# Second block of a two-block kernel: latent projections, rotations and gate tiles stand beside the attention steps, and masked key chunks are left out

## What is computed

```python
h = rmsnorm(x, pre_norm_mix)
g_a, g_b, qa, ka, va, cq, ckv, kr = split(h @ w_in)        # 1024,1024,512,128,128,256,128,32
out_a = attention_a(qa, ka, va, positions, sinks)          # 8 heads of 64, 2 key heads, window 128, ALiBi, sinks
qb  = rmsnorm(cq,  q_a_norm)  @ w_q_b                      # 8 heads of 64 + 32 (rotated)
kvb = rmsnorm(ckv, kv_a_norm) @ w_kv_b                     # 8 heads of 64 keys + 64 values
out_b = causal_attention(qb, kvb, rope(kr))                # 8 heads
merged = sigmoid(g_a) * (out_a @ w_o_a) + sigmoid(g_b) * (out_b @ w_o_b)
x = x + rmsnorm(merged @ w_out, post_norm_mix)
x = x + rmsnorm(relu(rmsnorm(x, pre_norm_mlp) @ w_up)**2 @ w_down, post_norm_mlp)
```

## Time and profile before

| what | value |
|---|---|
| median of 3 runs | 1555.5 us (1555.41 to 1556.49) |
| the profiled execution | 1553.86 us, of it the span 1552.1 us |
| TensorE matmul busy | 1351.1 us (87%) |
| VectorE busy | 998.1 us (64%) |
| ScalarE busy | 546.2 us (35%) |
| GpSimd busy | 628.8 us (41%) |
| mean granted TensorE clock | 0.946 of full speed |

### The profile page before, as it was taken

The page is one execution under the profiler, slowest core; times in us unless marked ns, Lnnn a source line. Parts: engine busy times, 40 slices in busy tenths (PEclk is TensorE's granted clock), DMA queues, the critical chain, the costliest instruction groups (busy, mean ns, idle before and its releaser), DMA issues. The chain is left out here.

```text
span 1552.1 us, 26715 instructions
## 1 busy us (share of the span) xinstructions
PE 1351.1 (87%) x10416; PEld 1296.6 (84%) x10416; DVE 998.1 (64%) x2056; ACT 546.2 (35%) x984; POOL 628.8 (41%) x361
## 2 busy tenths in 40 slices
PE   7989998899898878696888787888898898799996
PEld 6989998898897878696878787888886678689996
DVE  4698946755478585858585859555647565584563
ACT  6444454444432121211112121211564464344341
POOL 1387742221365545454545454542147312122220
PEclk9999999899999989898989898999999999899998
DMA  7445452442359999999999999999342224145450
GB/s 289 148 163 189 172 200 95 163 163 102 114 232 420 422 421 422 422 422 421 422 421 421 420 421 422 422 421 421 139 138 82 82 104 141 50 156 202 164 190 27
DMA packets 58073, 397.56 MB, mean 256 GB/s; under 512 B 6272, under 2 KB 9856, under 8 KB 10368
## 3 DMA queue, kind: packets, MB, share of 16 engines
q0 software_dynamic: 36864, 268.45, 41.6%
q1 hardware_dynamic: 21120, 127.89, 23.2%
HBM read 395.27 MB, written 1.05 MB: 255 GB/s over the span
## 5 line engine op out<-in xcount | busy, mean ns | idle before, releaser
L449 POOL TENSOR_TENSOR w_lo<-raw,w_hi 128x2048 fp32r<-128x2048 f32 x62 | 287.2, 4634 | 570.8 <-ACT w_hi L903 524.2
L761 PE MATMUL bank<-h_norm,rows_late 128*128 128x128 f32 x2816 | 332.8, 281 | 27.1 <-ACT h_norm L1052 27.1
L761 PEld LDWEIGHTS bank<-h_norm,rows_late 128*128 128x128 f32 x2816 | 328.6, 198 | 30.5 <-ACT h_norm L1052 30.5
L1591 DVE SCALAR_TENSOR_TENSOR rows_late<-rows_late,squares 128x1024 f32<-128x1024 f32 x176 | 212.8, 1223 | 131.0 <-DMA rows_late<-peer_uv_dram,stage 129.3
L588 PE MATMUL bank<-x_hi_a,w_hi 128*128 128x256 f32 (+1 forms) x904 | 266.5, 295 | 20.0 <-DVE x_lo_a L1214 11.0
L589 PE MATMUL bank<-x_lo_a,w_hi 128*128 128x256 f32 (+1 forms) x904 | 258.9, 286 | 0.0
L590 PE MATMUL bank<-x_hi_a,w_lo 128*128 128x256 f32 (+1 forms) x904 | 258.9, 286 | 0.0
L761 PE MATMUL bank<-h_norm,rows_early 128*128 128x128 f32 x1280 | 179.5, 309 | 91.0 <-ACT h_norm L1052 90.9
L761 PEld LDWEIGHTS bank<-h_norm,rows_early 128*128 128x128 f32 x1280 | 173.2, 222 | 97.6 <-ACT h_norm L1052 97.6
L530 POOL DMA_INDIRECT rows_late<-peer_uv_dram,stage x165 | 195.1, 1183 | 132.7 <-PE bank L761 95.1
L903 ACT ACTIVATE w_hi<-raw 128x2048 fp32r<-128x2048 f32 (+1 forms) x119 | 224.3, 1887 | 52.7 <-PE bank L590 45.7
...
## 6 DMA issues: line engine op xcount, KB each, us to landing
...
```

The lines of the kernel that those rows point to most:

```text
L449: api.tensor_tensor(ring(w_lo, i), ring(raw, i), ring(w_hi, i).bitcast(F32), ALU.subtract).then_inc(w_lo_ready[LO_BY[i][0]], 1)
L761: mm = nc.tensor.matmul(ct(Y_ACC[c][t // 4], t % 4, P), expert_rows(k)[:, D + t * P:D + (t + 1) * P], ct(diag, k % DIAGS, P), start=False, ...
L1591: w_.scalar_tensor_tensor(out=row, in0=row, scalar=1.0, in1=h_tok[:, c * D:(c + 1) * D], op0=ALU.mult, op1=ALU.mult, accum_out=pre[:, side ...
```

## The change

1. **Masked keys.** Scores, bias, exponentials and probabilities cover 384 columns instead of 512: 128 keys for the first token chunk, 256 for the second (`SEEN`, `SEEN_BY`). Three transposes instead of four; the second value matmul has 128 columns instead of 256.
2. **Order.** The attention loop starts after the first two `qa` tiles. Beside it stand, by step: 0 `ckv`, `kr`; 1 the other two `qa`; 2 the mean square of the key latent and `cq`; 3 `kn`, `vb`; 4 the mean square of the query latent, the rotation of `kr` and two gate tiles; 5 `qb`; 6 to 9 two query rotations each; 6 to 15 one gate tile each; 16 to 18 the last four gate tiles. The two mean squares are output tiles now, and their roots (`root_of_lora`) stand among the exponentials.
3. **Normalising.** ScalarE multiplies the probabilities by the inverse sums (`normalise`) instead of VectorE (L1459).
4. **Low parts.** VectorE makes the low parts of all weight blocks from `ka` up to the last gate block; 9 of them were GpSimd's. GpSimd keeps the ALiBi bias.
5. **Residual.** Scaling the second token chunk's residual (L1681, L1637) moves from the start of the block to step 15.

```diff
+SEEN = 3 * P
...
+ROTATED = {6: 0, 7: 2, 8: 4, 9: 6}
+GATE_TILES = {4: (0, 1), 16: (12, 13), 17: (14,), 18: (15,), **{i: (i - 4,) for i in range(6, 16)}}
...
-    p.append(("w_in_2_tail", 0, [("ckv", 0), ("kr", 0)], "act"))
-    add("w_in_2", [11], "cq", 2, "act")
-    add("w_in_2", [8, 9], "qa", 2, "act")
-    p.append(("w_kv_b_2", 0, [("kn", i) for i in range(HB)] + [("vb", i) for i in range(4)], "act"))
-    other("krot", 1, "dve")
-    p.append(("w_q_b_2", 0, [("qb", i) for i in range(HB)], "act"))
+    add("w_in_2", [8], "qa", 2, "act")
     for i in range(HA + HB + 3):
         if i >= 3:
             other(("apv", "bpv")[(i - 3) // HA], 1, "dve", (i - 3) % HA)
-        if i < HB:
-            other("qrot", 1, "dve", i)
-        if i % 2 == 0 and i < 16:
-            add("w_in_2", [i // 2], ("ga", "gb")[i // 8], 2, "act", i % 8)
+        if i == 0:
+            p.append(("w_in_2_tail", 0, [("ckv", 0), ("kr", 0)], "act"))
+        elif i == 1:
+            add("w_in_2", [9], "qa", 2, "act", 2)
+        elif i == 2:
+            other("kv_square", 1, "act")
+            add("w_in_2", [11], "cq", 2, "act")
+        elif i == 3:
+            p.append(("w_kv_b_2", 0, [("kn", h) for h in range(HB)] + [("vb", n) for n in range(4)], "act"))
+        elif i == 4:
+            other("q_square", 1, "act")
+            other("krot", 1, "dve")
+        elif i == 5:
+            p.append(("w_q_b_2", 0, [("qb", h) for h in range(HB)], "act"))
+        elif i in ROTATED:
+            other("qrot", 2, "dve", ROTATED[i])
+        for t in GATE_TILES.get(i, ()):
+            if t % 2 == 0:
+                split[gate_tile(t + 1)] = "w_in_2", t // 2
+                p.append(("w_in_2", t // 2, [gate_tile(t)], "act"))
+            else:
+                p.append((None, 0, [gate_tile(t)], "act"))
...
-            + [("w_in_2", b) for b in (2, 3, 4, 5, 6, 7, 11)])
-BY_DVE = range(LOAD_OF["pq", 12], BEFORE_GATHERS + 3)
+            )
+BY_DVE = range(LOAD_OF["pq", 12], LOAD_OF["gb", 7])
...
-            wait_tile(pool, "ka", 0)
...
-                subtract_to(BEFORE_ATTENTION + (u - XH) // 2)
...
+                g.tensor_scalar(seen(alibi, u), dist[:], -float(2.0 ** (-(h + 1.0) * 8.0 / HA)), None,
...
+            def scores(u):
+                kind, h = UNITS[u]
+                if UNITS[u - 2][0] == "x":
+                    pe.wait_ge(s_exp, NC * (u - 1))
+                else:
+                    pe.wait_ge(s_front, u - 1)
...
+                for c in range(NC):
+                    mm = nc.tensor.matmul(SCORE[u % 2][:, SEEN_BY[c]], q[:, c * P:(c + 1) * P], k[:, 0:(c + 1) * P],
+                                          start=True, stop=True)
+                mm.then_inc(s_ready, 1)
+            def transpose_probs(u):
+                pe.wait_ge(p_ready, u + 1)
+                pe.wait_ge(pt_copied, u - 1)
+                for n in range(3):
+                    mm = nc.tensor.transpose(ct(TRANS[u % 2], n, P), ct(seen(probs, u), n, P), ident)
+                mm.then_inc(pt_ready, 1)
+            def sum_values(u):
...
+                nc.tensor.matmul(out[r, 0:SEQ], values[:, at:at + width], pt[:, 0:SEQ], start=True, stop=False)
+                nc.tensor.matmul(out[r, P:SEQ], values[:, row + at:row + at + width], pt[:, SEQ:SEEN],
+                                 start=False, stop=True).then_inc(acc_ready, 1)
...
+            def lora_stat(name, kt, ones, first):
+                out = open_tile(name, 0)
+                for k in range(kt):
+                    pe.wait_ge(lora_squared, first + k + 1)
+                    mm = nc.tensor.matmul(out[:, 0:SEQ], ones[:], ct(lora_squares, first + k),
+                                          start=(k == 0), stop=(k == kt - 1))
+                mm.then_inc(acc_ready, 1)
...
+            def beside_attention(i):
+                if i == 0:
+                    linear("ckv", range(1), "w_in_2_tail", 0, "h2", DT, P + ROPE)
+                    linear("kr", range(1), "w_in_2_tail", 0, "h2", DT, P + ROPE, lo=P, rows=ROPE)
+                elif i == 1:
+                    linear("qa", range(2, 4), "w_in_2", 9, "h2", DT, 256)
+                elif i == 2:
+                    lora_stat("kv_square", 1, mean_kv, 0)
+                    linear("cq", range(2), "w_in_2", 11, "h2", DT, 256)
+                elif i == 3:
+                    latent_keys_values()
+                elif i == 4:
+                    lora_stat("q_square", 2, mean_q, 1)
+                    wait_drained(pe, "kr", 0)
+                    out = open_tile("krot", 0)
+                    nc.tensor.matmul(out[0:QHB, 0:SEQ], rot, k_r[NOPE:QHB, :], start=True, stop=True).then_inc(acc_ready, 1)
+                elif i == 5:
+                    latent_queries()
+                elif i in ROTATED:
+                    for h in (ROTATED[i], ROTATED[i] + 1):
+                        out = open_tile("qrot", h)
+                        wait_drained(pe, "qb", h)
+                        nc.tensor.matmul(out[0:QHB, 0:SEQ], rot, ct(q_b, h)[NOPE:QHB, :],
+                                         start=True, stop=True).then_inc(acc_ready, 1)
+                for t in GATE_TILES.get(i, ()):
+                    name, n = gate_tile(t)
+                    linear(name, [n], "w_in_2", t // 2, "h2", DT, 256, lo=(t % 2) * P)
...
+            for i in range(HA + HB + 3):
+                u = XH + i
+                if i < HA + HB:
...
+                    scores(u)
+                if 2 <= i < HA + HB + 2:
+                    transpose_probs(u - 2)
+                if i >= 3:
+                    sum_values(u - 3)
+                beside_attention(i)
...
+            def exponents(u):
+                act.wait_ge(s_front, u + 1)
...
+            def normalise(u):
+                act.wait_ge(inverse_ready, u - XH + 1)
+                for c in range(NC):
+                    at = NC * (u % 2) + c
+                    p_c = seen(probs, u)[:, SEEN_BY[c]]
+                    ins = s.activation(p_c, p_c, ACT.Copy, scale=row_inv[:, at:at + 1])
+                ins.then_inc(p_ready, 1)
+            def copy_transposed(u):
+                act.wait_ge(pt_ready, u + 1)
+                if u >= XH + 2:
+                    kind, h = UNITS[u - 2]
+                    wait_tile(act, PV_TILES[kind], h)
+                s.activation(seen(probs_t, u), TRANS[u % 2][:, 0:SEEN], ACT.Copy).then_inc(pt_copied, 1)
...
+            def root_of_lora(name):
+                wait_tile(act, name, 0)
+                s.activation(root_buf[:], acc(name, 0), ACT.Sqrt, bias=eps[:, 0:1]).then_inc(acc_freed["act"], 1)
+            def beside_attention(i):
...
+                elif i == 2:
+                    root_of_lora("kv_square")
+                    split_hi("kv", 0, lambda k: act.wait_ge(lora_normed, 1), c_kv[:])
+                    for n in range(2):
+                        drain("cq", n, ct(c_q, n))
+                    for n in range(2):
+                        wait_drained(act, "cq", n)
+                        s.activation(ct(lora_squares, 1 + n), ct(c_q, n), ACT.Square).then_inc(lora_squared, 1)
+                elif i == 3:
+                    for h in range(HB):
+                        ahead("kn", h)
+                        wait_tile(act, "kn", h)
+                        s.activation(ct(k_b, h)[0:NOPE, :], acc("kn", h)[0:NOPE, :], ACT.Copy).then_inc(acc_freed["act"], 1)
+                    for c in range(NC):
+                        for half in range(2):
+                            drain("vb", 2 * c + half, v_b[:, c * D + half * 512:c * D + (half + 1) * 512], width=512)
+                elif i == 4:
+                    root_of_lora("q_square")
+                    for n in range(2):
+                        split_hi("q", n, lambda k: act.wait_ge(lora_normed, 2 + k), ct(c_q, n))
+                elif i == 5:
+                    wait_drained(act, "krot", 0)
+                    for h in range(HB):
+                        s.activation(ct(k_b, h)[NOPE:QHB, :], k_r[NOPE:QHB, :], ACT.Copy).then_inc(rope_ready, 1)
+                    for h in range(HB):
+                        ahead("qb", h)
+                        wait_tile(act, "qb", h)
+                        s.activation(ct(q_b, h)[0:QHB, :], acc("qb", h)[0:QHB, :], ACT.Copy).then_inc(acc_freed["act"], 1)
...
+            for i in range(HA + HB + 3):
+                u = XH + i
+                if i < HA + HB:
+                    exponents(u)
+                if 1 <= i <= HA + HB:
+                    normalise(u - 1)
+                if 2 <= i < HA + HB + 2:
+                    copy_transposed(u - 2)
+                beside_attention(i)
...
+            def front(u):
...
+                link(w_.scalar_tensor_tensor(out=p_u, in0=SCORE[u % 2][:, 0:SEEN], scalar=scale, in1=bias,
+                                             op0=ALU.mult, op1=ALU.add))
+                for c in range(NC):
+                    tok = done(w_.tensor_reduce(maxima[:, c:c + 1], p_u[:, SEEN_BY[c]], AX, ALU.max), dve_step)
```

(35 more changed lines are left out.)

408 lines of the change are left out of this document (187 added, 221 removed).

## The result

| | before | changed |
|---|---|---|
| median | 1556.04 us (8 runs, 1555.41 to 1560.46) | 1562.58 us (8 runs, 1558.60 to 1562.76) |
| profiled execution, its span | 1553.86, 1552.1 us | 1562.52, 1560.7 us |
| mean granted TensorE clock | 0.946 | 0.938 |
| first matmul of the block, us from the start | 1107.29 | 1108.97 |
| from there to the first `oa` matmul | 159.2 us | 165.3 us |

The ratio is 1.0034, with an interval of 1.0024 to 1.0045: slower by 0.34%, where I had forecast 4 us gained. The range ended at 1562, so it missed as well.

A forecast was written before the change was run, and what follows sets the result against it. TensorE was taken to bound the stretch from the block's first matmul to `oa`. Removing 28.4 us and adding 24.3 gave 4.1 us gained: 1555.5 - 4.1 = 1551.4 us, with an 8-in-10 range of 1541 to 1562.

The forecast's parts named there:

- narrower steps: All 16 heads: fewer masked columns in scores, transposes and value products save TensorE 0.55 us a head, 8.8 us.
- chain one: End of step 2's scores to first `kn` tile read out: 17.7 us serial; TensorE waits about 7.5 us.
- chain two: Start of step 4 to first `qb` copy: 21.9 us serial; TensorE waits about 7.5 us.
- slow clock behind the chains: After the two new idle times: TensorE slows, 3.0 us charged twice, 6.0 us; bounds 0 and 12.
- late steps, waits: From step 10: VectorE's low part ahead of the next front makes TensorE wait, 3.0 us; bounds 0 and 8.
- old waits and slow stretches: Before `oa`: 13.5 us idle, two slow stretches of 4.9 and a `kn` stall of 1.2 go.
- The residual: Step 16: its scaling, moved to step 15, stands ahead of the last inverse sums, some 2 us late.
- Nine blocks' low parts leave GpSimd: Loop: 20.6 us more for VectorE, paid by L1459's absence and 45 us idle, apart from the chains.
- The multiplication on ScalarE: Each head: taken as 0.55 us, near a copy; held twice in each chain; ends move each -0.3 to +1.5.
- The rule on table loads: Before the roots: the skill's drain of about 1.38 us a load would add 2.8 us; the trace spoke against it.
- TensorE stays at its slow level: Rival, steps 3 to 6: low clock lasts, 16 us replace 6, 1561 us, slower; chance 0.17.
- blocked beside GpSimd's bias: On the chains: VectorE's operations held, like a negation of 1.98 us instead of 0.2, adding 1.8 each.

The follow-up runs named there:

- 8: The kernel before with TensorE's part of the masked keys alone; VectorE and ScalarE still handle 512 columns: 1554.5 us.
- 11: The changed kernel with all latents before the loop, one gate tile a step, gate low parts behind the next front, `k_r` copies one a step: 1536.7 us.
- 1: The changed kernel with the low parts of the last six gate blocks on GpSimd again: 1546.5 us.
- 6: The changed kernel with VectorE's gate-block low parts from step 6 on behind the next step's front and inverse sums instead of ahead: 1549.5 us.
- Experiment 10: The kernel of 6 with VectorE's low parts of steps 2 and 4 also behind the next step's front and inverse sums: 1544.1 us.
- Experiment 3: The changed kernel with the probabilities multiplied by the inverse sums on VectorE again instead of ScalarE: 1551.8 us.
- Experiment 2: The changed kernel with the residual's scaling behind step 16's inverse sums instead of ahead of them in step 15: 1561.7 us.
- experiment 12: The kernel of 11 with the multiplication by the inverse sums on VectorE: 1535.8 us.
- experiment 4: The changed kernel with the smaller block of `ckv` and `kr` second in order again and its tiles ahead of the loop: 1559.6 us.

## Why the prediction was wrong, step by step

Forecast of the stretch to `oa`: 159.2 - 28.4 + 24.0 = 154.8 us. Measured: 165.3.

| term | forecast | measured | shown by |
|---|---|---|---|
| narrower steps | -8.8 | -8.5 | 8: 0.53 a head |
| chain one | +7.5 | +7.6 | timeline |
| chain two | +7.5 | +8.2 | timeline |
| slow clock behind the chains | +6.0 | +5.1 | last four `kn` tiles with `vb` 6.8 us (1157.79 to 1164.57), last four `qb` tiles 5.4 (1187.92 to 1193.28); in 11, at the full level, 4.25 and 2.9 |
| late steps, waits | +3.0 | +7.0 | 1 and 6 |
| late steps, slow clock | 0 | +4.9 | 6 |
| old waits and slow stretches | -19.6 | gone | no wait of that form before step 10 |
| not placed | | +1.4 | |

- **The steps that held.** The two chains came out as chained, within 0.7 us in sum, with table loads directly before both roots. Their composition was not mine: at the fifth tile, where I had put some 7 us each, TensorE waits 2.48 and 5.56 us. The rest stands at earlier tiles, most of it (3.23 and 2.18) at the fourth, for VectorE's copy of a head's output, which I had not seen as a link. The sums held because the last wait ends with the chain, and the chains were nearly as long as I had them: the fifth `kn` tile begins 18.7 us after step 2's scores (17.7 forecast), the fifth `qb` tile 23.3 us after step 4's start (21.9 forecast). Experiment 10 shows that this wait hung on the low part ahead of the front, as the chain has it, and that ScalarE's order follows right behind.
- **The step that failed** is "I take 3.0 us in all; bounds 0 and 8" for the steps from 10 on, together with the charge of slow stretches for two idle times only. I had the mechanism (a low part ahead of the next front in even steps) and sized it from one step alone: multiplied probabilities 11.3 us after the step's start, wanted after 10.4. They came after 13.3 us from step 10 (1217.95 to 1231.27) and 14.6 from step 14 (1241.95 to 1256.57), and were wanted after 11.0 and 11.5: the waits of 2.4 and 3.2. Three links were missing or short. ScalarE multiplies behind the next head's exponentials (0.98 us from 1254.90 to 1255.88); with the durations of the prediction the front alone ends at 10.0 us, so 11.3 has no room for exponentials (1.3) and multiplication (0.55) behind it. In step 10, head 10's front begins when VectorE has finished step 9's rotations, while the transposes that it must follow were over at 1219.57:

```profile
1220.06 0.42 DVE L1820 TENSOR_TENSOR q_b<-q_b,turns 32x256 f32<-32x256 f32 x1
1220.52 0.56 DVE L1574 SCALAR_TENSOR_TENSOR probs<-bank,const 128x384 f32<-128x384 f32 x1
...
1225.84 2.29 DVE L478 TENSOR_TENSOR w_lo<-raw,w_hi 128x2048 fp32r<-128x2048 f32 x1 [3.26 <-ACT w_hi L981]
...
1230.49 0.78 ACT L1046 ACTIVATE probs<-probs,row_inv 128x128 f32<-128x128 f32 x2
```

  And `oa`'s high and low parts in step 13 (1.33 and 1.43 us) push head 14's front to 1245.82, so the chain that ends in step 16 starts late. Experiment 3 bears on the first link (late waits 4.3 us instead of 7.0). The other two are read from the timeline, and no run moves them. Waits of 2.4 and 3.2 us were also followed by a granted clock of 0.71 and 0.50; four stretches, not two. Both together are 11.9 us where I had 3.0, and 8.9 us turn a gain of 4 into a loss of 5.
- **The residual.** I laid 2 us of step 16's wait on it. Experiment 2 shows zero.
- **"Nine blocks' low parts leave GpSimd" and are paid "by VectorE's idle 45 us".** The idle time was there, and experiment 6 uses it. A busy share says nothing about where in the program the work stands; the same 2.3 us ahead of a front cost 11.9 us in all and behind it nothing.
- **The multiplication on ScalarE.** I compared the durations (0.55 against the copy's 0.4 to 0.5; it took 0.69 for the pair) and not the places in the queues. Experiment 3 prices the move at 9.5 us in this order, and experiment 12 at nothing in the order of experiment 11.
- **The price of the order.** Masked keys were worth 8.5 us of work. Experiment 11 gets 21 us out of the stretch of the kernel before with the latents ahead of the loop; the changed kernel spent 15.8 + 5.1 us to put them in.
- **The rule on table loads.** The load before the first root takes 1.28 us and starts 0.01 us after the copy ends, the root 0.02 after the load:

```profile
1143.07 0.47 ACT L1055 ACTIVATE squares<-bank 128x384 f32<-128x384 f32 x1
1143.55 1.28 ACT L1213 ACT_TABLE_LOAD   x1
1144.85 0.47 ACT L1213 ACTIVATE root_buf<-bank,eps 128x256 f32<-128x256 f32 x1
```

  So the trace shows no pause beside the load, and the 2.8 us by the Trainium skill (ScalarE: Activation LUTs, What ACT_TABLE_LOAD costs) would have been right in direction and wrong in cause.
- **The rivals.** "TensorE stays at its slow level" came nearest in time (1561), but the clock comes back within each of the four steps; "blocked beside GpSimd's bias" was not seen on the chains. Its ground was misread as well: the negation of 1.98 us (1164.93 to 1166.91) stood beside a low part on GpSimd (1162.39 to 1166.89), not beside a bias, and the changed kernel has no low part there. The block's first matmul at 1108.97 instead of 1107.29 I can't place: experiment 4 does not tie it to the larger block, and the scatter of 5 us between kernels covers it. The medians differ by 6.5 us, the spans of the two profiled executions by 8.6: 1.7 ahead of the block, 6.1 in the stretch to `oa`, 0.9 behind it (0.3 forecast).
